# A two-block transformer kernel: two weight slabs of the second block fetched in four row parts each

## The reference

```
for l in range(DEPTH):                         # second_block, DEPTH = 2
    xn = rmsnorm(x, norm_mix[l]); proj = xn @ w_in[l]
    ... five mixers; the fifth is memory_attention(u_mem, mem, mem_norm[l], w_mem_kv[l], ...)
    x = x + cat @ w_out[l]
    x = x + peer_ffn(rmsnorm(x, norm_ffn[l]), peer_wq[l], peer_subkeys[l], peer_u[l], peer_v[l])

peer_ffn:  for every token and each of 8 heads, the 16 best of 128 x 128 experts:
    act = gelu(sum_d u_tab[i] * xn);  out += softmax(best) * act * v_tab[i]
memory_attention:  kv = rmsnorm(mem, mem_g) @ w_kv    # does not depend on x
```

## Time and profile before

| | |
|---|---|
| Time, median of 3 runs | 3102.86 us (3102.05 to 3104.77) |
| Profiled execution | 3100.25 us, span 3098.4 us |
| TensorE busy | 2912.1 us (94%) |
| VectorE busy | 2065.2 us (67%) |
| DMA of POOL's queue (gathers) | 536.90 MB, 41.8% of 16 engines' span |
| DMA of SP's queue | 282.74 MB, 25.6% |
| Layer 0's expert stage | from about 1654 to 2314 us |
| Granted TensorE clock | 0.999 |

### The profile page before, as it was taken

One profiled execution on the slowest core, in us unless ns is written; L12 is line 12 of the kernel. 1 busy time (PEld: TensorE's weight loads), 2 busy tenths in 40 slices (PEclk: granted clock), 3 DMA queues, 4 the chain that ended last, 5 costly groups with the idle time before them and its releaser, 6 DMA issues.

```text
span 3098.4 us, 37421 instructions
## 1 busy us (share of the span) xinstructions
PE 2912.1 (94%) x14096; PEld 1921.4 (62%) x14096; DVE 2065.2 (67%) x4826; ACT 636.5 (21%) x1588; POOL 579.5 (19%) x554
## 2 busy tenths in 40 slices
PE   8999999999999999999999988888989998888877
PEld 8957887895985888798675433333438553333322
DVE  7753532775774633477577877777756797777775
ACT  1113221110101223021262211112125321111110
POOL 0010000000001000000012433333321253333332
PEclk9999999999999999999999999999999999999999
DMA  6444324454454333355457999999995799999998
GB/s 235 176 170 138 115 96 136 171 183 163 173 182 157 129 110 109 136 200 223 148 206 304 419 421 421 421 417 417 414 384 190 290 421 421 421 421 421 421 421 334
DMA packets 119124, 831.60 MB, mean 268 GB/s; under 512 B 13344, under 2 KB 15904, under 8 KB 19744
## 3 DMA queue, kind: packets, MB, share of 16 engines
q0 software_dynamic: 73728, 536.90, 41.8%
q1 hardware_dynamic: 43632, 282.74, 25.6%
q10 hardware_dynamic: 1584, 9.56, 0.9%
HBM read 828.10 MB, written 1.05 MB: 268 GB/s over the span
## 4 chain that ended last, share of the span: by engine, by line
PE 60%; DMA 27%; DVE 7%; issue 4%; ACT 1%; POOLq 0%; DVEq 0%; SPq 0%; ACTq 0%
DMA arena<-table_uv,idx 23%; PE bank L499 12%; PE bank L559 9%; PE bank L398 6%; PE bank L2649 5%; PE bank L730 5%; PE bank L486 5%; DMA ring<-table_uv,idx 4%; PE bank L2332 3%; PE bank L973 3%; PE bank L425 2%; PE bank L2520 1%; DVE arena L3334 1%; DVE diag L3342 1%; PE bank L2367 1%
## 5 line engine op out<-in xcount | busy, mean ns | idle before, releaser
L2649 PE MATMUL bank<-arena,diag 128*128 128x512 f32 x1704 | 837.5, 614 | 128.6 <-DVE diag L3342 122.1
L3334 DVE CUSTOM_DVE_ANT_0 arena<-arena 128x1024 f32<-128x1024 f32 x426 | 520.6, 1222 | 211.3 <-DMA arena<-table_uv,idx 208.5
L2649 PEld LDWEIGHTS bank<-arena,diag 128*128 128x128 f32 x1704 | 291.3, 189 | 559.1 <-DVE diag L3342 352.7
L3435 POOL DMA_INDIRECT arena<-table_uv,idx x426 | 422.4, 991 | 767.7 <-PE bank L2649 566.4
L2909 ACT ACTIVATE dots<-dots 128x1 f32<-128x1 f32 x512 | 103.6, 203 | 1067.6 <-DVE dots L3334 1065.6
L1891 POOL TENSOR_TENSOR x_tok<-arena,ktail 128x1024 f32<-128x1024 f32 (+1 forms) x10 | 22.6, 2259 | 1477.2 <-ACT arena L1002 1477.2
L2649 PE MATMUL bank<-ring,diag 128*128 128x512 f32 x344 | 169.6, 615 | 31.1 <-DVE diag L3342 30.1
L486 PE MATMUL bank<-x,ring 128*128 128x128 f32 x1408 | 173.3, 277 | 9.6 <-DMA ring<-stream 9.3
L3342 DVE TENSOR_SCALAR diag<-cst,dots,soft 128x128 f32<-128x128 f32 x512 | 175.8, 344 | 5.6 <-ACT dots L2909 5.5
L730 PE MATMUL bank<-x,ring 128*128 128x256 f32 x768 | 174.6, 381 | 0.0
L486 PEld LDWEIGHTS bank<-x,ring 128*128 128x128 f32 x1408 | 165.8, 194 | 11.2 <-issue 8.4
(11 more groups left out here) (695 smaller groups left out, 4451.9 us busy)
## 6 DMA issues: line engine op xcount, KB each, us to landing
ring<-stream SPq DMA_DIRECT2D x240, 1024.0 KB, 4.9
arena<-table_uv,idx POOLq DMA_INDIRECT x426
ktail<-ln_rows ACTq DMA_DIRECT2D x6, 1024.0 KB, 5.0
arena<-stream SPq DMA_DIRECT2D x4, 1024.0 KB, 8.1
arena<-mem_rows SPq DMA_DIRECT2D x2, 1024.0 KB, 9.7
more<-stream SPq DMA_DIRECT2D x2, 1024.0 KB, 8.7
cst<-stream SPq DMA_DIRECT2D x2, 1024.0 KB, 7.1
sq<-keys ACTq DMA_DIRECT2D x2, 1024.0 KB, 4.8
```

The costliest lines, as they stand in the source:

```text
L2649: last = mm(bank[4 + 2 * tt + half][:, :], diag[:, n % DIAGS, :], row_slot(l, n)[:, D + 512 * half:D + 512 * half + 512], start=(h == 0 an ...
L3334: v.tensor_tensor_reduce(u, u, tok[:, tt, :], 1.0, 0.0, ALU.mult, ALU.add, dots[:, tt, k:k + 1]).then_inc(u_used.sem, 1)
L3435: g.indirect_dma_start(out=row_slot(l, n), out_offset=None, in_=peer_uv, in_offset=bass.IndirectOffsetOnAxis(ap=idx[:, h % 2, tt, k:k + 1] ...
```

## The change

Slabs 16 and 17 (`in_parts`) are each fetched by four DMAs, of partitions 0 to 39, 40 to 79, 80 to 119 and 120 to 127. All other slabs are fetched as before. Each of the four adds 16 to the slot's semaphore, so that the value TensorE waits for is now counted by `loads`.

```diff
+ROW_PARTS = ((0, 40), (40, 80), (80, 120), (120, P))
...
+        in_parts = (SLABS2 + S_MEMK, SLABS2 + S_MEMV)
+
+        def loads(n):
+
+            return sum(len(ROW_PARTS) if m in in_parts else 1 for m in range(n % RING2, n + 1, RING2))
+
         def fetch(sp, n):
             sp.wait_ge(slab_done.sem, n + 1)
-            sp.dma_start(ring[:, n % RING2].rearrange("p b n -> p (b n)"),
-                         stream[n // SLABS2 * STREAM2 + n % SLABS2]).then_inc(slab_loaded[n % RING2], 16)
+            to, src = ring[:, n % RING2].rearrange("p b n -> p (b n)"), stream[n // SLABS2 * STREAM2 + n % SLABS2]
+            for lo, hi in ROW_PARTS if n in in_parts else ((0, P),):
+                sp.dma_start(to[lo:hi, :], src[lo:hi, :]).then_inc(slab_loaded[n % RING2], 16)
...
             def slab(l, s):
 
                 n = l * SLABS2 + s
-                pe.wait_ge(slab_loaded[n % RING2], 16 * (n // RING2 + 1))
+                pe.wait_ge(slab_loaded[n % RING2], 16 * loads(n))
                 return ring[:, n % RING2]
```

## The result

The changed kernel takes 3113.82 us (median of 7 runs, 3111.10 to 3116.65), the one before 3102.05 us (7 runs, 3101.74 to 3104.77). The ratio is 1.0036, with an interval of 1.0027 to 1.0046: slower by 11.8 us, where 2.3 us was forecast and the range ended 4.8 us above the median. The profiled execution took 3116.65 us, span 3114.7 us.

A forecast was written before the change was run, and what follows sets the result against it. From about 1722 us the DMA engines' rate was taken as the bound. Issues and semaphore cost 0; unequal shares put loaded engines 3.1 us behind, between 2.2 and 3.1 remain: 3102.86 + 2.3 = 3105.2 us, range 3101.0 to 3107.7.

The forecast's parts named there:

- The issues and the semaphore: SP issuing eight DMAs instead of two, and TensorE's higher semaphore count for the slabs: each forecast to cost 0.
- How the rows are dealt to the engines: Slab fetch: parts on 10, 10, 10 and 8 engines give loaded ones 10 rows more over two slabs, 3.1 us.
- When it hits: Start of the stage: gather 1 lands 2.2 us later, adding to DVE's 2.91 us wait at product 1.
- What is given back: Around the gather issued at 1695.81: idle time absorbs only the excess of 3.1 over 2.2 us; 2.3 us remain.
- Rival A: Slab fetch: parts dealt evenly or over changing engines, so nothing moves; 3102.9 us, up to 3104.1; chance 15%.
- Rival B: Slab fetch: the engine that lags at the stage's end is spared rows; -1.9 us, 3101.0 us; chance 12%.
- Rival C: Slab fetch: slower than forecast, eight engines take all, 3107.9 us, or rows collide, 3106 and up; chance 13%.

The follow-up runs named there:

- r64: Both slabs in two DMAs of 64 partitions each, against the kernel before: 3109.62 us, ratio 1.0021.
- r32: Both slabs in four DMAs of 32 partitions each, against the kernel before: 3111.29 us, ratio 1.0029.
- fix2: Whole slabs, issued only when product 1 of the stage is done, against the kernel before: 3103.48 us, ratio 1.0001.
- late_whole: Whole slabs, issued only when product 99 of the stage is done, against the kernel before: 3104.75 us, ratio 1.0006.
- late_parts: The change's parts, issued only when product 99 is done: 3118.51 us, ratio 1.0052 against the kernel before.
- cols: Both slabs in four DMAs each of all 128 partitions and 512 of 2048 columns, against the kernel before: 3103.04 us, ratio 1.0001.
- alone_mid64: Slabs in parts of partitions 0 to 31, 32 to 95, 96 to 127, first gather held until both landed, against the kernel before: 3109.54 us, one run.
- mid64: Both slabs in DMAs of partitions 0 to 31, 32 to 95 and 96 to 127, against the kernel before: 3108.69 us, ratio 1.0018.
- alone_r64: Both slabs in two DMAs of 64 partitions, first gather held until both landed, against the kernel before: 3112.27 us, one run.

## Why the prediction was wrong

*The issues and the semaphore* cost 0, as forecast. SP's eight issues took 4.81 us, and its next wait was 658.4 us long.

*How the rows are dealt to the engines* is the step that failed. Its count was right: 76 small packets in SP's queue, 44 more packets in the page (43,676 against 43,632), so ten, ten, ten and eight engines. Its price was wrong. It took the 0.311 us of a row as a constant of the engine, and so could only charge for the additional rows on the loaded ones, 2.3 us in all. But the runs show 0.31 us only where the rows written at one time lie on both sides of partition 64 (whole slabs, the middle parts) or a fetch has just begun. With parts of 40 the engines crowd, a slab's row takes 0.534 us, and, which no term of the sum had, the gathers' rows beside them rise from 0.34 to 0.55 us. For 24 us the rate is 236 GB/s in place of 421, and that alone is 10.5 us. r64 shows the size of this with the count of rows unchanged: 6.8 us. The 5.0 us from there to 11.8 hold what the unequal shares cost, 3.1 us by the forecast's count; with r32 as the start, also with equal shares, it is 3.4 us. No run split these further, so that what unequal shares cost by themselves stays open.

*When it hits* was the right place with the wrong size. DVE's wait at product 1 is not 5.1 us but 7.49 us, and product 0 has one of 7.43 us before it, where the forecast gave product 0 at most 2 us. The chain from there is as forecast: product 1, TensorE's row and the gather behind the pause are all late by the same amount (+11.95, 26.01 us apart as before, +11.88).

*What is given back* came out as forecast, nothing, but the reason was only half of it. The forecast argued that an engine behind schedule stays behind since the chain carries the delay. fix2 and late_whole show that the chain is not what counts: with product 1 and gather 15 3 us sooner than before, the stage ends no sooner. The DMA engines' total work sets the stage's length, and late_parts pays as much (13.8 us) at a place where the chain has passed. Had the reasoning been from throughput, the question would have been: at what rate do these 2.1 MB and what runs beside them move?

*Rival A* (nothing moves) fell. *Rival B* (the spared engine is the slow one) could not have shown beside a loss of this size; which engine lags stays open. *Rival C* named "rows of one engine collide with another's", said that nothing in the rows spoke for it, and priced it at 3106 us and up; that is the mechanism, with 3% for more than 6 us. The rows before show no part DMA at all, so nothing spoke against it either, and the range stopped at 3107.7: of all the bounds only this one had no row beneath it. Rival C's other price, parts dealt to four or five engines, 10 to 14 us, would have hit the time by luck. The 76 small packets (ten for each part of 40) exclude it, and so does r64, where all 16 engines share.

What is not settled: whether the source side, where the slabs are read, has a share. cols and the middle part of alone_mid64 speak against it, no kernel tried it by itself. That mid64 is cheaper than r64 rests on its traces (8.6 against 10.5 us alone), not on its times. Of the map in W, only the two sides of partition 64 are shown. No version ran that beats the kernel before: cols, fix2 and before are the same within the interval.

## What to carry to other kernels

A DMA that covers only some partitions is not a piece of the whole one: it can run at half of the rate (221 of 421 GB/s in alone_r64) and slows what the other queue moves beside it, so if a load is to be fetched in parts, cut its columns and leave all partitions in each part (cols: ratio 1.0001). Where DMA bandwidth sets a stage's length, count MB and rate over the stretch, not the wait that ends last: the lost GB/s come out as lost time wherever they fall.

## What the hardware showed that I had not expected

- A DMA share of 1.0 says nothing of the rate: 187, 221, 239, 308 and 421 GB/s all occurred at a share of 0.99 to 1.06. Two numbers of one window row have to be read together.
- Transfers in two queues hurt one another beyond their own bytes: the gathers' rows, to all 128 partitions, took 0.55 us on average beside the parts and 0.34 us beside whole slabs.
- The same two slabs cost about as much deep in the stage (13.8 us) as at its start (11.8 us).
- Four column parts of 2 KB a row, four times the packets, moved with no measurable cost (ratio 1.0001).
